# A norm factor applied late in the router, a second place used once for expert chunks, and one expert chunk loaded during the recurrence

## The reference

```
x' = rmsnorm(x)
P  = x' @ W_in
x  = x + W_out( sigmoid(G_a) * P_a(HGRN2(x')) + sigmoid(G_b) * P_b(RWKV7(x')) )
x  = x + MoE_top4of32(rmsnorm(x) * norm2_w)
y  = rmsnorm(x) * final_norm_w
```

```
logits = rmsnorm(x) @ router_w + router_b          # 1024 x 32
top_val, top_idx = top_k(logits, 4); gates = softmax(top_val)
h   = rows @ w_gu[e] + b_gu[e]                     # 1024 x 2048 for each expert
act = glu * sigmoid(1.702 * glu) * (lin + 1)       # clamped at 7
out = act @ w_down[e] + b_down[e]                  # 1024 x 1024 for each expert
x  += sum of gates * out
```

## Time and profile before

| what | us |
|---|---|
| median of 3 runs | 1377.87 |
| range of these runs | 1377.36 to 1379.27 |
| the profiled execution, its own time | 1377.52 |
| its span | 1375.7 |
| TensorE busy | 1325.3 |
| VectorE, ScalarE, GpSimd busy | 373.6, 245.8, 68.0 |
| bytes moved | 449.38 MB |

### The profile page before, as it was taken

One profiled execution on the slowest core, in us unless ns is written; L12 is line 12 of the kernel. 1 busy time (PEld: TensorE's weight loads), 2 busy tenths in 40 slices (PEclk: granted clock), 3 DMA queues, 4 the chain that ended last, 5 costly groups with the idle time before them and its releaser, 6 DMA issues.

```text
span 1375.7 us, 18547 instructions
## 1 busy us (share of the span) xinstructions
PE 1325.3 (96%) x7381; PEld 635.2 (46%) x7381; DVE 373.6 (27%) x990; ACT 245.8 (18%) x534; POOL 68.0 (5%) x138
## 2 busy tenths in 40 slices
PE   8999999999999999999999999999999999999997
PEld 6778668888756333333333333333323333233332
DVE  3335654443243511211212112121121121121112
ACT  3153333222112101111111011110111011011112
POOL 7000310000033000000000000000000000000000
PEclk9999999999999999999999999999999999999999
DMA  8431623101469899999999999999999999999995
GB/s 245 147 114 40 215 62 100 32 32 63 149 214 405 324 412 426 428 428 429 429 429 428 430 429 429 429 429 430 429 430 430 429 429 429 429 429 430 429 429 219
DMA packets 62902, 449.38 MB, mean 327 GB/s; under 512 B 4980, under 2 KB 33590, under 8 KB 38184
## 3 DMA queue, kind: packets, MB, share of 16 engines
q1 hardware_dynamic: 55874, 441.24, 77.5%
q0 software_dynamic: 1552, 4.87, 1.4%
q10 hardware_dynamic: 5430, 2.62, 0.7%
HBM read 443.95 MB, written 4.76 MB: 326 GB/s over the span
## 4 chain that ended last, share of the span: by engine, by line
PE 73%; DMA 21%; DVE 3%; ACT 2%; issue 1%; ACTq 0%; SPq 0%; DVEq 0%
DMA ring<-in_expert_w_gu_dram 21%; PE bank L1101 20%; PE bank L1135 12%; PE bank L455 9%; PE bank L1023 5%; PE bank L1054 4%; PE bank L559 3%; PE bank L962 2%; PE bank L932 2%; ACT arena L1161 1%; PE bank L827 1%; PE bank L811 1%; PE bank L1096 1%; PE bank L1030 1%; PE bank L813 1%; PE bank L501 1%
## 5 line engine op out<-in xcount | busy, mean ns | idle before, releaser
L1101 PE MATMUL bank<-ring,arena 128*64 128x512 f32 x1520 | 340.6, 595 | 10.9 <-DMA ring<-in_expert_w_gu_dram 10.9
L1101 PEld LDWEIGHTS bank<-ring,arena 128*64 128x64 f32 x1520 | 106.1, 137 | 219.0 <-issue 178.8
L1161 ACT ACTIVATE arena<-bank 128x512 f32<-128x512 f32 (+5 forms) x227 | 115.4, 525 | 482.6 <-PE bank L1135 205.8
L1135 PE MATMUL bank<-ring,arena 128*64 128x512 f32 x768 | 171.8, 596 | 0.0
L1161 ACT ACTIVATE arena<-arena 128x256 f32<-128x256 f32 (+5 forms) x102 | 61.1, 607 | 494.7 <-DVE arena L2029 486.4
L2029 DVE TENSOR_SCALAR arena<-bank 128x256 f32<-128x256 f32 x64 | 27.0, 421 | 384.6 <-PE bank L1101 384.6
L1101 PE MATMUL bank<-arena 128*64 128x512 f32 x528 | 119.4, 594 | 4.6 <-DMA arena<-in_expert_w_gu_dram 3.7
L455 PE MATMUL bank<-arena,ring 128*128 128x288 f32 (+1 forms) x464 | 118.2, 415 | 0.5 <-ACT arena L1161 0.5
L2051 DVE COPY arena<-bank 64x512 f32<-64x512 f32 x32 | 22.2, 694 | 340.3 <-PE bank L1135 340.3
L455 PEld LDWEIGHTS bank<-arena,ring 128*128 128x128 f32 x464 | 88.5, 192 | 29.5 <-issue 3.1
L1135 PEld LDWEIGHTS bank<-ring,arena 128*64 128x64 f32 x768 | 52.4, 137 | 97.1 <-issue 94.4
(11 more groups left out here) (348 smaller groups left out, 1137.6 us busy)
## 6 DMA issues: line engine op xcount, KB each, us to landing
ring<-in_expert_w_gu_dram SPq DMA_DIRECT2D x95, 2048.0 KB, 28.4
ring<-in_expert_w_down_dram SPq DMA_DIRECT2D x48, 2048.0 KB, 33.5
arena<-in_expert_w_gu_dram SPq DMA_DIRECT2D x33, 2048.0 KB, 29.8
arena<-in_expert_w_down_dram SPq DMA_DIRECT2D x16, 2048.0 KB, 34.0
ring<-in_w_in_dram SPq DMA_DIRECT2D x23, 1024.0 KB, 5.1
ring<-in_w_out_dram SPq DMA_DIRECT2D x4, 1024.0 KB, 9.1
ring<-in_state_hgrn_dram POOLq DMA_DIRECT2D x1, 2048.0 KB, 12.3
out_dram<-ring ACTq DMA_DIRECT2D x1, 2048.0 KB, 9.4
```

The source lines that it names most:

```text
L1101: ins = mm(bank[q % 2][64 * (q // 2):64 * (q // 2) + 64, :], gu_lhs(c), w[:, q * 512:(q + 1) * 512], start=(c == 0), stop=(c == KT - 1), s ...
L1135: ins = mm(bank[1][64 * h:64 * h + 64, :], dn_lhs(j, r), w[:, r * D + h * 512:r * D + (h + 1) * 512], start=(j == 0 and r == 0), stop=(j = ...
L1161: return nc.scalar.activation(out, in_, f, **kw)
```

## The change

The diff makes three changes.

1. Norm factor late. For tile 1, VectorE multiplies a half of the columns by the norm weight as soon as that half of W_out is done (`last_rows`), transposes, evacuations and logits go on with rows that lack the factor, and the factor is applied to the 32 logits of a row. ScalarE scales `x2` itself afterwards (`rstd` 7), and TensorE waits for that before it picks rows. The squares of tile 1 are split to the same halves. The logits of tiles 2 and 0 are made as four partial sums of 32 partitions each (`part_logits`), evacuated, and folded by a product with a constant matrix (`fold_logits`); this is placed between the products of W_out's last half. Filler products: 3, 8 and 6 instead of 2, 8 and 8. Memsets of `GT` and `yo` go; three one-element memsets raise their semaphores.
2. A tenth place, also used once (`ONCE` = 2), by chunk 9, over the second norm's weights, the parameters and the first buffers of stage 2. The router's buffers move behind it, and the final norm's weights are loaded in front of chunk 18.
3. Chunk 1 is loaded at piece 21 of W_in (`EARLY`), once HGRN2's states and outputs are done. Its place overlaps scratch of HGRN2 and RWKV-7, so buffers of RWKV-7 move: `yaT` lies over the prompt's HGRN2 state and waits for its output, the squares lie over the norm weights, and with that the second norm's and the router's weights are loaded after `ob_done` 5.

The core of the diff:

```
-WS = 8
+WS, ONCE = 8, 2
...
-        yaT, Qm = HR[:, 0:512], HR[:, 512:1024]
+        yaT, Qm = HR[:, 2560:3072], HR[:, 3072:3584]
...
+                if n == EARLY:
+                    sp.wait_ge(S("hg_state"), 8)
+                    sp.wait_ge(S("hg_o_evac"), 3)
+                    w_load(sp, 0, 1, True)
...
+            sp.wait_ge(S("ob_done"), 5)
+            sp.dma_start(norm_bc, norm2_w.partition_broadcast(P)).then_inc(S("norm_loaded"), 16)
...
-            for s in (0, 1, 2, 3, 5):
+            for s in (0, 2, 3, 5):
...
-            sp.wait_ge(S("logits"), 3)
+            sp.wait_ge(S("logits"), 2)
             w_load(sp, 1, WS, True)
-            for s in range(WS + 1, QUAD * ECH):
-                sp.wait_ge(w_used, s - WS + (s > 2 * WS))
+            sp.wait_ge(S("xn_done"), 7)
+            sp.wait_ge(S("rstd"), 6)
+            w_load(sp, 1, WS + 1, True)
+            for s in range(WS + ONCE, QUAD * ECH):
+                if s == 2 * WS + ONCE:
+                    sp.wait_ge(w_used, WS + ONCE)
+                    sp.dma_start(norm_bc, final_norm_w.partition_broadcast(P)).then_inc(S("norm_loaded"), 16)
+                sp.wait_ge(w_used, s - WS - ONCE + 1 if s < 2 * WS + ONCE else s - WS + 1)
                 w_load(sp, s // ECH, s, True)
...
+            def part_logits():
+
+                for (o, rows), c in ((TILES[0], 0), (TILES[2], P)):
+                    for kt in range(KT):
+                        g = NE * (kt % 4)
+                        i = mm(bank[6][g:g + NE, c:c + rows], rw_sb[:, kt * NE:(kt + 1) * NE], x2T[:, kt * NT + o:kt * NT + o + rows],
+                               start=(kt < 4), stop=(kt >= 4), skip_group_check=True)
+                done(i, "x2T")
...
+            x2_T(2, bank[6:7])
...
+            x2_T(0, bank[0:2])
+            w_out_tile(1, acc(1)[1:2], 0, 3)
...
+            part_logits()
+            w_out_tile(1, acc(1)[1:2], 3, 5)
+            pe.wait_ge(S("x2T_evac"), 4)
+            fold_logits()
+            pe.wait_ge(S("xn_done"), 6)
+            x2_T(1, bank[0:1], 0, 4)
+            w_out_tile(1, acc(1)[1:2], 5, KT)
+            pe.wait_ge(S("x2T_evac"), 5)
+            last_logits(0, 4)
+            pe.wait_ge(S("xn_done"), 7)
+            x2_T(1, bank[6:7], 4, KT)
+            keep_busy(3)
+            pe.wait_ge(S("x2T_evac"), 6)
+            done(last_logits(4, KT), "logits")
             keep_busy(8)
...
                 act.wait_ge(S("rw_T"), 2 * u + 1)
+                if u == 0:
+                    act.wait_ge(S("hgrnp_out"), 16)
...
+            def last_rows(h):
+
+                out, c = acc(1)[h]
+                dve.wait_ge(S("wo_done"), 3 + h)
+                step(v.tensor_tensor(x2[:, 1, c], out, norm_bc[:, c], ALU.mult), "xn_done")
...
+            choose(2)
+            last_rows(1)
+            choose(0)
+            dve.wait_ge(S("rstd"), 6)
+            dve.wait_ge(S("logits"), 2)
+            step(v.scalar_tensor_tensor(out=lg[:, NE:2 * NE], in0=logit_cols(1), scalar=st3[:, 13:14], in1=rb_bc, op0=ALU.mult, op1=ALU.add))
+            choose(1)
...
-            g.memset(GT, 0.0).then_inc(S("gt_evac"), 1)
-            for x in range(2):
-                g.memset(yo[:, x * 512:(x + 1) * 512], 0.0).then_inc(S("y_evac"), 1)
```

More of the change, by code:

```diff
@@ L974, in x2_T, with fold_logits, last_logits @@
                         done(i, "x2T")
-            def logits(t):
-                o, rows = TILES[t]
-                out = logit_cols(t)
-                for kt in range(KT):
-                    i = mm(out[0:rows, :], x2T[:, kt * NT + o:kt * NT + o + rows], rw_sb[:, kt * NE:(kt + 1) * NE],
+            def part_logits():
[5 more added lines that the diff above has]
+                done(i, "x2T")
+            def fold_logits():
+                for t, c in ((0, 0), (2, P)):
+                    rows = TILES[t][1]
+                    i = mm(logit_cols(t)[0:rows, :], part[:, c:c + rows], fold, start=True, stop=True)
+                done(i, "logits")
+            def last_logits(k0, k1):
+                o, rows = TILES[1]
+                for kt in range(k0, k1):
+                    i = mm(logit_cols(1), x2T[:, kt * NT + o:kt * NT + o + rows], rw_sb[:, kt * NE:(kt + 1) * NE],
                            start=(kt == 0), stop=(kt == KT - 1))
-                done(i, "logits")
+                return i
             def keep_busy(n):
@@ new lines, in _ @@
+            residual_norm(2, (1, 1))
+            residual_norm(0, (2, 2))
+            x2_evac(2, 1, bank[6], 0)
+            x2_evac(0, 2, bank[0], 0)
+            x2_evac(0, 3, bank[1], 4)
+            act.wait_ge(S("x2T"), 4)
+            done(fn(part, bank[6][:, 0:P + NS], ACT.Copy), "x2T_evac")
+            residual_norm(1, (3, 4))
+            act.wait_ge(S("rstd"), 6)
+            for h in range(2):
+                c = slice(h * 512, (h + 1) * 512)
+                i = fn(x2[:, 1, c], x2[:, 1, c], ACT.Copy, scale=st3[:, 13:14])
@@ L1927, in _, with choose @@
             k4 = [P, 3, TOPK, NE]
[L1928 to L1931 removed]
+            def choose(t):
+                e8 = slice(8 * t, 8 * t + 8)
                 step(v.max(v8[:, e8], lg[:, NE * t:NE * (t + 1)]))
@@ L1937, in _ @@
                 step(v.tensor_reduce(M[:, t * NE:(t + 1) * NE], M4[:, t].rearrange("p k e -> p e k"), AX.X, ALU.add), "chosen")
+            dve.wait_ge(S("logits"), 1)
+            for t in (2, 0):
+                rows = TILES[t][1]
+                i = v.tensor_tensor(lg[0:rows, t * NE:(t + 1) * NE], logit_cols(t)[0:rows, :], rb_bc[0:rows, :], ALU.add)
+            step(i)
+            choose(2)
[3 more added lines that the diff above has]
+            dve.wait_ge(S("logits"), 2)
@@ new lines, in _ @@
+            step(v.scalar_tensor_tensor(out=selc[0:NS, 2:3], in0=bank[0][0:NS, P + 64:P + 65], scalar=1.0, in1=M0[0:NS, 2:3],
+                                        op0=ALU.add, op1=ALU.mult))
+            dve.wait_ge(S("bgu3"), 1)
+            for t, (o, rows) in enumerate(TILES):
+                i = v.tensor_scalar(sel[0:rows, t * SLOTS:(t + 1) * SLOTS], ramp[0:rows, 0:SLOTS], 1.0, selc[0:rows, t:t + 1], ALU.add, ALU.is_equal)
+            step(i, "sel_ready")
+            v.tensor_copy(Rk[:, 0:64], bank[0][:, P:P + 64])
@@ L2175, in _ @@
             pool.wait_ge(S("rw_end"), 1)
+            step(g.memset(fold, 0.0))
+            for x in range(4):
+                i = sel(fold[NE * x:NE * x + NE, :], ALU.not_equal, 0, [[-1, NE]], 1, 1.0)
+                step(i)
             step(g.memset(lg, 0.0))
```

140 lines of the change are left out of this document (66 added, 74 removed).

## The result

The changed kernel takes 1382.03 us (median of 11 runs, 1380.21 to 1385.91); the kernel before, run on the same chips, takes 1378.31 us (11 runs, 1375.56 to 1380.74). The ratio is 1.0028 (95% interval 1.0016 to 1.0039), some 3.9 us slower. The forecast was 1377.2 us and no change that can be told; the time lies 1.2 us above the range of 1373.0 to 1380.8, on the side of rival 3. The profiled execution took 1381.89 us, its span is 1380.1.

A forecast was written before the change was run, and what follows sets the result against it. The chunk stream was taken to set the end, its unpaused stretch starting from TensorE's use of chunk 10. 1377.52 - 3.2 (router) + 2.5 (output delay) = 1376.8 us profiled, 1377.2 as median with 0.35 added; range 1373.0 to 1380.8.

The forecast's parts named there:

- rival 3: Slower: stop at 227 us (3.6 us) and clock fall (1.4) exceed the router's 1.85 us gain; 1381.0 us, chance 13%.
- What bounds the kernel: Expert stage: chunk stream at 429 GB/s sets the end, starting from TensorE's use of chunk 10; 174 chunks x 4.89 us.
- The router: Last tile's router: late norm factor, dropped memsets and fillers at full clock bring chunk 10 3.2 us earlier (1.85 if clock falls).
- The clock: Granted clock: taken as full at the router; a fall after the recurrence's stop priced at 1.4 us, in rival 3 only.
- The two places: Chunk stream before chunk 18: tenth place and early chunk make room for the 3.2 us, without which 2.1 us is lost.
- Rival 2: Chunk stream before 505 us: places worth what they carry, up to 2 x 4.9 us; 1368 to 1373 us, chance 12%.
- The pause before chunk 18: Sign in the profile: the chunk stream pauses some 6 us before chunk 18 is issued.
- Where the early chunk is issued: Start of the recurrence, 221 us: loads delay the HGRN state's output, stopping ScalarE and TensorE; delay 2.5 us reaches chunk 10.
- The landing: HGRN state's output beside chunk and W_in piece lands at 228.5 us; landing up to 226.0 costs nothing.
- the upper bound of 230.0: Latest landing of the HGRN state's output, ending with both loads: 221.25 + 0.9 + 4.9 + 2.4 + 0.6; delay 4.0 us.
- The ratio of 1.5 to 1: Output packets against load packets, from 254 to 164 in 376 to 378 us: 12 per engine pass beside the chunk.
- the main case: Whole kernel: router gain and output delay nearly cancel, 1377.2 us, own range 1375.5 to 1379.5, chance 50%.

The follow-up runs named there:

- e1: Changed kernel with the early chunk issued only once the prompt's HGRN2 state output has landed: 1376.1 us, ratio 0.998 to the kernel before.
- e2: Changed kernel with the 1 MB piece of W_in queued ahead of the early chunk instead of behind it: 1376.45 us, ratio 0.9989 to the kernel before.
- e3: Changed kernel without the early chunk (chunk 1 loaded with chunks 0, 2, 3 and 5, as before): 1374.29 us, ratio 0.997 to the kernel before.
- e5: Changed kernel with 20 filler products in front of TensorE's wait near 227 us: 1379.78 us, ratio 1.0011 to the kernel before.
- e6: e1 with the gate and up bias products moved from before the seventh to before the eighth product of an expert: 1372.64 us, ratio 0.996 to before.
- e7: e1 without the three filler products behind the router's last transposes: 1374.38 us, ratio 0.9973 to the kernel before.
- e10: Changed kernel without the early chunk, the 1 MB piece of W_in issued at the moment of the state's output: 1373.05 us, one timed run.
- e11: Kernel before with only the gate and up bias products moved in front of the eighth product: 1377.07 us, ratio 0.9995 to the kernel before.
- e9: Changed kernel with the 1 MB piece of W_in held until the state's output has landed, only the chunk beside it: 1386.56 us, one timed run.
- e8: e1 with the tenth place not used ahead (nine chunks ahead, as before): 1375.84 us, ratio 0.9985 to the kernel before.
- e4: e3 with chunk 9 held until chunk 0 is used (nine chunks ahead), the late norm factor alone: 1376.35 us, ratio 0.9988 to the kernel before.

## Why the prediction was wrong

**What bounds the kernel: right.** From the issue of chunk 18 to the end the table gives 872.3 to 872.7 us for the kernel before, the changed one and e1, e2, e3, e5, e6, e7 and e10 (e11 873.1, e9 873.7; where places lack, e8 873.5 and e4 874.6). 429 GB/s and 25 us of waits for chunks stayed.

**The router: right.** Foretold 3.2 us, measured 3.37 (3.4 in e1, free of the other parts). With the 8.11 us taken off: logits 437.8 (437.9 foretold), choice 439.7 (439.7), ranks 439.7 (439.9). The clock stayed at 1.00, as taken; the reason given for it (hardly a gap) didn't hold in e7. The five steps behind W_out add to 3.2 us, not to the 3.3 of the working, which changes nothing.

**The two places: right.** They "make room (...) and give nothing else": without room the end is 2.0 us later (e4; 2.1 foretold), the tenth place alone gives all of it (e3), and the early chunk adds nothing to it (e1 against e3). Rival 2 is out. The pause before chunk 18 was 4.5 us, with "some 6" foretold.

**Where the early chunk is issued: the step that failed.** The mechanism was named: output and loads share the engines, ScalarE waits, TensorE waits, and the delay reaches chunk 10 undiminished. Its term, 2.5 us, measured 8.1: 5.7 for the landing and 2.4 for the clock.

*The landing.* Foretold 228.5, seen at 231.7, later even than the upper bound of 230.0. The queues of the changed kernel in 227 to 228 and in 229 to 230 us:

```profile
q1 hardware_dynamic: 30, 0.49, 117.6%
q10 hardware_dynamic: 30, 0.02, 5.3%
...
q1 hardware_dynamic: 237, 0.24, 67.9%
q10 hardware_dynamic: 231, 0.12, 38.5%
```

The first pair is the chunk's 16 KB packets beside the output's of 0.5 KB, the second the piece's of 1 KB beside them: one for one, whatever the size. By 228, 126 of the chunk's 128 packets had started and 110 of the output's 512. But the landing was set by one engine that was behind the others. The third queue in 226 to 228 us, and the two queues in 230.3 to 231.2:

```profile
q8 instruction: 1, 0.02, 2.8%
...
q1 hardware_dynamic: 333, 0.34, 106.4%
q10 hardware_dynamic: 14, 0.01, 2.5%
```

On fifteen engines the output was through by 230.3. Then its last packets start one by one, 66 ns apart, until 231.13, and the signal's packet follows at 231.20. Against the working, on this last engine: the chunk was through at 229.6 and not at 227.0 (2.6 us); 24 packets, and not 20, took 1.5 us beside the piece and not 1.1 (0.4 us); the signal took 0.5 us, with 0.4 foretold (0.1 us). That is 3.1 of the 3.2 us.

The first part has two sources. The chunk was slow at its start: its 12 packets of 222 to 223 took 102.9% of 16 engines' microsecond, 1.4 us for one, where those of 227 to 228 took 0.63. And on the last engine its last packet started at 228.97, on the others by 228.07, 0.9 us earlier. The trace names no engine for a packet, but the times fit together. The packet of queue q8, kind instruction, 16 KB, runs from 226.93 to 227.81; an output packet at 227.80 takes 71 ns instead of 27, and a packet of the chunk at 227.85 takes 1.10 us instead of 0.61. The same row of three is in e5 (from 224.94) and e9 (from 230.52), and in e2 such a packet runs from 227.10. In all four the last engine passes the end of the output 0.9 to 1.0 us behind the others. No run leaves this packet out, so it is inferred from the times. Without it the landing would be at about 230.8 (an estimate, 231.7 less the 0.9), still above the bound.

The time of a packet could have been had from the kernel before. There the output's took 27 ns (166 in 56.9% of 16 engines' half microsecond, 222 to 222.5) and the piece's 47 (674 in 208 to 210, which they filled), so a pair takes 75 ns of an engine, and 24 pairs 1.8 us. The working had priced these packets by their bytes at the full rate. The bound failed for the same reason, besides the chunk's slow start and the last engine: it added bytes at 429 GB/s, and in 229 to 230 the two queues moved only 0.36 MB.

What the working said of the landing's price held: all up to 226.0 for nothing, each microsecond after that a microsecond of TensorE. Counted from the issue, e10 landed 1.1 us past that point and its products came 1.2 us late, e2 2.7 and 2.8, the changed kernel 5.6 and 5.7.

The ratio of 1.5 to 1 was a misreading of the earlier trace rows besides: it foretold 12 packets for an engine beside the chunk, where there were 8. The same queues of the kernel before, in halves of a microsecond, 376 to 376.5 and 377.5 to 378:

```profile
q1 hardware_dynamic: 49, 0.20, 95.5%
q10 hardware_dynamic: 48, 0.01, 10.8%
...
q1 hardware_dynamic: 21, 0.05, 23.0%
q10 hardware_dynamic: 108, 0.02, 22.8%
```

While both had work they took turns one for one there too; the 254 to 164 came from the last half microsecond, in which the loads ran out. The Trainium skill (DMA: Bandwidth & Descriptors, section "Queues, rings and completion order") says that a DMA engine takes turns between its queues a packet at a time. These rows agree, with a single packet of the profile for each turn. The section gives a packet as typically 9 to 17 descriptors; how the profile's packets stand to descriptors no row tells, but turns of so many of them there are none here: 30 packets over 16 engines are two for an engine in the microsecond.

*The clock.* It was priced for rival 3 alone, at 1.4 us; the main case puts it at nothing without a word. For the stop that the main case foretold, 2.5 us, nothing was right: after the 2.6 us of e2 and the 1.0 us of e10 the granted clock was 1.00. After the 5.5 us of the changed kernel it was 0.50 until 238, after the 4.6 us of e9 0.50 until 242, and with fillers in e5 it stayed at 1.00. So the clock's term came with the landing's error and not beside it. Its price in the changed kernel is 2.4 us by its own trace (8.1 less 5.7) and 2.1 to 2.2 against e5; in e9 it was 3.2.

**Rival 3: right in kind.** "It decides as soon as the output lands after about 229": it landed at 231.7. Its sum of 1381.0 is near the 1382.0 measured, with a smaller stop and clock (3.6 and 1.4, measured 5.7 and 2.4) and a smaller gain of the router (1.85, measured 3.4). The errors of 3.1 and 1.55 us partly cancel, so that its number came so near is luck. By measured terms, 1377.52 - 3.4 + 8.1 = 1382.2; the profiled execution took 1381.89. It had 13%, because the bound at 230.0 made it look as though all had to go wrong at once.

**Still open.** Why the output's packets start 2 to 3 us late when a load is issued in the same moment; why the signal of e2 took 1.1 us where the others took 0.4 to 0.5; whether the instruction packet is what holds the last engine up; and what sets off the low clock in the router of the order before.

## What to carry to other kernels

A load put beside a small output doesn't cost the output its share of the bytes but a turn for each packet: count packets, not bytes, read the two queues in stretches so short that neither runs dry, and take the time of a packet from its own row. A wait that holds TensorE idle is priced with the low clock behind it: waits of 4.6 and 5.5 us had it here, waits of 1.0 to 2.6 us didn't. Where an output's memory is to be used again soon, send the big load when it has landed: here 2.4 us of patience in a load that nobody waits for gave back 8 us.

## What the hardware showed that was not expected

- The packets of two queues passed one for one whatever their size: 0.5 KB beside 16 KB, 30 to 30; 0.25 KB beside 4 KB, 48 to 49; 0.5 KB beside 1 KB, 231 to 237.
- One of the 16 engines passed the output 0.9 to 1.0 us behind the others in four traces (changed kernel, e2, e5, e9). Its times fit those of one 16 KB packet of kind instruction, which took 0.88 us in each; that it is the cause is inferred.
- An output issued alone had its first packets within 1 us; beside a load of about a thousand packets of 1 KB issued in the same moment it had them 2.8 to 2.9 us after its issue (e2, e10), beside one of 128 packets of 16 KB after 2.0 to 2.2 us (changed kernel, e5, e9).
- After 5.5 us without work the granted clock was 0.50 for 5 us of work and cost 2.1 to 2.4 us, after 4.6 us without work (e9) 0.50 for 6.4 us of work, 3.2 us; after waits of 2.6 us (e2) and 0.75 us (e7) it was 1.00.
- The clock in the router of the kernel before fell for about 3 us in one trace and to 0.50 for over 8 us in another (e11), in the same order of work up to that place; in the eleven traces of the new order it was 1.00.
